# First layer's gated feed-forward: down products summed with tokens on partitions, and the embedding projection moved ahead of the gate

## The reference

```python
def gated_conv_ffn(u, w_up, conv_w, conv_b, w_down):
    up = u @ w_up
    a, g = up[..., :D_FF_2], up[..., D_FF_2:]
    a = causal_depthwise_conv(a, conv_w, conv_b)
    return (jax.nn.gelu(a, approximate=False) * g) @ w_down

    # one layer of the second block, D_FF_2 = 2816, PLE_DIM = 256
        u = rms_norm(h, attn_norm_w[i])
        proj = u @ w_in[i]
        ...
        h = h + mixed @ w_out[i]
        h = h + gated_conv_ffn(rms_norm(h, ffn_norm_w[i]), w_up[i], conv_w[i], conv_b[i], w_down[i])
        gate = jax.nn.sigmoid(rms_norm(h, ple_norm_w[i]) @ w_ple_gate[i])
        h = h + gate * (p[i] @ w_ple_proj[i])
```

## Time and profile before

| | value |
|---|---|
| median of 3 runs | 1278.66 us (1278.36 to 1279.01) |
| the profiled execution's own time | 1278.2 us |
| span from its first to its last instruction | 1276.5 us |
| granted TensorE clock, mean | 0.999 of 2.4 GHz |
| PE, DVE, ACT busy | 99%, 73%, 53% of the span |
| memory read | 228 MB, 180 GB/s over the span |

### The profile page before, as it was taken

The page is one execution under the profiler, slowest core; times in us unless marked ns, Lnnn a source line. Parts: engine busy times, 40 slices in busy tenths (PEclk is TensorE's granted clock), DMA queues, the critical chain, the costliest instruction groups (busy, mean ns, idle before and its releaser), DMA issues.

```text
span 1276.5 us, 20241 instructions
## 1 busy us (share of the span) xinstructions
PE 1267.4 (99%) x7932; PEld 1123.8 (88%) x7932; DVE 931.8 (73%) x1143; ACT 681.6 (53%) x808; POOL 32.6 (3%) x60
## 2 busy tenths in 40 slices
PE   9999999999999999999999999999999999999997
PEld 8988888888998888887889999999988898999996
DVE  5757765667667756658887888777877968877784
ACT  6646444446565444446655654444665556544455
POOL 0000000000132000000000000000000000000000
PEclk9999999999999999999999999999999999999999
DMA  9635655555433655554553455455455535554530
GB/s 377 243 129 220 232 184 189 197 197 196 139 128 133 242 191 184 182 190 169 203 165 133 165 183 200 179 196 186 177 173 192 172 132 182 198 192 175 194 133 33
DMA packets 34550, 232.44 MB, mean 182 GB/s; under 512 B 4016, under 2 KB 4272, under 8 KB 7344
## 3 DMA queue, kind: packets, MB, share of 16 engines
q1 hardware_dynamic: 30960, 218.90, 48.0%
q10 hardware_dynamic: 3520, 12.55, 3.0%
HBM read 228.29 MB, written 1.05 MB: 180 GB/s over the span
## 4 chain that ended last, share of the span: by engine, by line
PE 99%; DVE 0%; issue 0%; ACT 0%; DVEq 0%; ACTq 0%
PE ring L435 23%; PE ring L431 12%; PE ring L340 7%; PE ring L342 7%; PE ring L341 7%; PE acc L522 5%; PE acc L524 5%; PE acc L523 5%; PE acc L340 5%; PE acc L341 5%; PE acc L342 5%; PE acc L435 2%; PE ring L522 1%; PE ring L461 1%; PE ring L524 1%; PE ring L523 1%
## 5 line engine op out<-in xcount | busy, mean ns | idle before, releaser
L332 DVE TENSOR_TENSOR wlo<-raw,whi 128x2048 fp32r<-128x2048 f32 x203 | 463.8, 2290 | 86.1 <-ACT whi L324 85.4
L324 ACT CAST whi<-raw 128x2048 fp32r<-128x2048 f32 x200 | 381.6, 1909 | 79.8 <-PE acc L342 31.3
L435 PE MATMUL ring<-xs,whi 128*128 128x512 f32 x1280 | 320.5, 392 | 0.0
L435 PEld LDWEIGHTS ring<-xs,whi 128*128 128x128 f32 x1280 | 230.2, 189 | 41.2
L431 PEld LDWEIGHTS ring<-xs,wlo 128*128 128x128 f32 x1280 | 172.6, 190 | 12.5 <-issue 1.7
L431 PE MATMUL ring<-xs,wlo 128*128 128x256 f32 x1280 | 180.2, 284 | 0.0
L340 PE MATMUL ring<-xs,whi 128*128 128x256 f32 x512 | 148.0, 289 | 0.1
L341 PE MATMUL ring<-xs,whi 128*128 128x256 f32 x512 | 144.8, 283 | 0.0
L342 PE MATMUL ring<-xs,wlo 128*128 128x256 f32 x512 | 144.8, 283 | 0.0
L340 PE MATMUL acc<-hhi,whi 128*128 128x256 f32 x368 | 104.2, 283 | 0.0
L342 PE MATMUL acc<-hhi,wlo 128*128 128x256 f32 x368 | 104.1, 283 | 0.0
(11 more groups left out here) (370 smaller groups left out, 1825.0 us busy)
## 6 DMA issues: line engine op xcount, KB each, us to landing
raw<-wstream SPq DMA_DIRECT2D x206, 1024.0 KB, 4.9
sq<-lnp ACTq DMA_DIRECT2D x3, 1024.0 KB, 5.0
hT<-xT ACTq DMA_DIRECT2D x4, 256.0 KB, 5.7
raw<-wstream SPq DMA_DIRECT2D x4, 256.0 KB, 5.4
raw<-wstream SPq DMA_DIRECT2D x2, 512.0 KB, 8.6
hT<-xtok ACTq DMA_DIRECT2D x1, 1024.0 KB, 18.1
misc<-decay ACTq DMA_DIRECT2D x1, 1024.0 KB, 4.9
kT<-lnp ACTq DMA_DIRECT2D x1, 1024.0 KB, 4.9
```

What stands on the lines that cost most here:

```text
L324: act.copy(whi[:, c % SPLIT, :], raw[:, c % RAW, :]).then_inc(hi_made, 1)
L332: dve.tensor_tensor(wlo[:, c % SPLIT, :], raw[:, c % RAW, :], whi[:, c % SPLIT, :].bitcast(f32), ALU.subtract).then_inc(lo_made, 1)
L435: mm = pe.matmul(to(b + t), wh[:, w], xs[:, k, :, :].rearrange("p a s -> p (a s)"), start=False, stop=k == NT - 1, skip_group_check=True)
```

## The change

In layer 0 alone, the down products use `rows_half` into the four `acc` banks with tokens on partitions. The first product of each bank starts the bank itself, so ACT's clearing copy is left out. After the last down chunk ACT copies each of the four banks to `v`, and TensorE turns them by 16 transposes of 128x128 into ring banks 0 to 3, from which DVE adds to `hT`. The transposes are woven into the last chunk's products: three quarters of the product, eight transposes, the last quarter, eight transposes. The projection chunk comes ahead of the four gate chunks in the weight stream and on TensorE. TensorE's loop over the steps is cut at another place (1, then 2 to 5 and 6 to 9, then 10). Layer 1 keeps its form. The order of the operations on DVE and ACT between the layers stays the same but for the sources and semaphores.

```diff
@@ -32,8 +32,9 @@
 C_IN = [C_B2 + PER_B2 * n for n in range(DEPTH)]
 C_OUT = [c + 14 for c in C_IN]
 C_FFN = [c + 18 for c in C_IN]
-C_GATE = [c + 3 * N_FF for c in C_FFN]
-C_PROJ = [C_GATE[0] + 3, C_GATE[1] + 3]
+C_POST = [c + 3 * N_FF for c in C_FFN]
+C_GATE = [C_POST[0] + 1, C_POST[1]]
+C_PROJ = [C_POST[0], C_POST[1] + 3]
 C_END = [C_GATE[1] + j for j in (0, 1, 2, 4)]
 N_CHUNKS = C_B2 + PER_B2 * DEPTH
 
...
@@ -604,6 +604,37 @@
                         mm.then_inc(acc_done, 1)
                 mm.then_inc(chunk_used, 1)
 
+            def down_rows(c, s, mc, first):
+
+                pe.wait_ge(lo_made, mc + (c + 1))
+                for t in range(2):
+                    for half in range(2):
+                        mm = rows_half(1, c, t, half, hhi[:, s, :, :], hlo[:, s, :, :], first, False)
+                mm.then_inc(chunk_used, 1)
+
+            def last_down_rows(c, s):
+
+                def product(t, half):
+                    return rows_half(1, c, t, half, hhi[:, s, :, :], hlo[:, s, :, :], False, True)
+
+                def turned(t, half):
+                    pe.wait_ge(rows_kept, 2 * t + half + 1)
+                    for f in range(4):
+                        o = bank(2 * half + f // 2)[:, (f % 2) * 256 + t * 128:(f % 2) * 256 + t * 128 + 128]
+                        mm = pe.transpose(o, v[:, t, half * 512 + f * 128:half * 512 + f * 128 + 128], ident)
+                        if t and f % 2:
+                            mm.then_inc(rows_turned, 1)
+
+                pe.wait_ge(lo_made, c + 1)
+                product(0, 0).then_inc(ff_rows, 1)
+                product(0, 1).then_inc(ff_rows, 1)
+                product(1, 0).then_inc(ff_rows, 1)
+                for half in range(2):
+                    turned(0, half)
+                product(1, 1).then_inc(chunk_used, 1)
+                for half in range(2):
+                    turned(1, half)
+
             def squares_sum(n, o):
 
                 pe.wait_ge(sq_summed, n + 1)
@@ -626,8 +657,8 @@
 
                 pe.wait_ge(lo_made, c + 1)
                 pe.wait_ge(p_lo, L + 1)
+                pe.wait_ge(rows_kept, 4)
                 for j in range(4):
-                    pe.wait_ge(y_made, 4 * (2 + 3 * L) + j + 1)
                     for k in range(2):
                         for t in (2 * j, 2 * j + 1):
                             w = slice(k * D + t * 128, k * D + t * 128 + 128)
@@ -726,17 +757,23 @@
                     pe.wait_ge(g_sum, m * 4 + (b + i))
                     wide_gemm(ca + 1, 2, mc=m * 12)
                     pe.wait_ge(prod_lo, m * 4 + (b + i))
+                    if L == 0:
+                        down_rows(ca + 2, (i - 1) % 2, m * 12, i == 1)
+                        return
                     if i == 1:
-                        pe.wait_ge(acc_zero, ZERO[f"ffn{L}"] + 1)
+                        pe.wait_ge(acc_zero, 1)
                     down(ca + 2, (i - 1) % 2, mc=m * 12)
 
-                with pe.Fori(0, (N_FF - 1) // 4) as m:
-                    for i in range(1, 5):
+                step(1)
+                with pe.Fori(0, (N_FF - 3) // 4) as m:
+                    for i in range(2, 6):
                         step(i, m)
-                for i in range(N_FF - 2, N_FF):
-                    step(i)
+                step(N_FF - 1)
                 pe.wait_ge(prod_lo, b + N_FF)
-                down(c0 + 3 * N_FF - 1, (N_FF - 1) % 2, last=True)
+                if L == 0:
+                    last_down_rows(c0 + 3 * N_FF - 1, (N_FF - 1) % 2)
+                else:
+                    down(c0 + 3 * N_FF - 1, (N_FF - 1) % 2, last=True)
 
             def head(h):
                 return slice(64 * (h % 2), 64 * (h % 2) + 64)
@@ -1080,11 +1117,11 @@
                 ffn(L, X + 2)
                 if L + 1 == DEPTH:
                     break
+                ple_projection(C_PROJ[L], L)
                 for j in range(3):
                     gemm(C_GATE[L] + j, j, X + 3 if j == 0 else None,
                          between=(lambda: squares_sum(3 * L + 2, bank(3)[:, 0:S])) if j == 2 else None)
-                ple_projection(C_PROJ[L], L)
-                last_gate(C_GATE[L] + 4, L)
+                last_gate(C_GATE[L] + 3, L)
 
             def gate_rows(j, ts=(0, 1), between=None):
 
...
@@ -1374,8 +1411,9 @@
                 split_hi(act, c0 + 1 + AHEAD)
                 g_crossed(c0 + 1, 0)
                 split_hi(act, c0 + 2 + AHEAD)
-                act.copy(acc[:, :, :].rearrange("p t s -> p (t s)").rearrange("p (a b) -> p a b", b=128),
-                         wide(maskadd[:, 128:256], 16)).then_inc(acc_zero, 1)
+                if L:
+                    act.copy(acc[:, :, :].rearrange("p t s -> p (t s)").rearrange("p (a b) -> p a b", b=128),
+                             wide(maskadd[:, 128:256], 16)).then_inc(acc_zero, 1)
                 gelu(0)
                 high(0)
 
@@ -1394,6 +1432,10 @@
                         step(i, m)
                 for i in range(N_FF - 2, N_FF):
                     step(i)
+                if L == 0:
+                    for n, (t, half) in enumerate(((0, 0), (0, 1), (1, 0), (1, 1))):
+                        act.wait_ge(*((ff_rows, n + 1) if n < 3 else (chunk_used, c0 + 3 * N_FF)))
+                        act.copy(v_rows(t, half), acc_bank(2 * t + half)).then_inc(rows_kept, 1)
 
             def load_exp_ln():
 
...
@@ -1683,13 +1725,13 @@
                     act.activation(z, z, ACT.Sigmoid).then_inc(sig_made, 1)
 
                 def next_high(j):
-                    act.wait_ge(*((gate_passed, 3 * L + j + 1) if j < 3 else (chunk_used, C_GATE[L] + 5)))
+                    act.wait_ge(*((gate_passed, 3 * L + j + 1) if j < 3 else (chunk_used, C_GATE[L] + 4)))
                     weighted_high(3 * L + 3, "attn_w", 8 * L + 8, j)
 
                 for j in range(3):
                     gate_sigmoid(j)
                 for j in (3, 4):
-                    split_hi(act, C_GATE[L] + j + AHEAD)
+                    split_hi(act, C_POST[L] + j + AHEAD)
                 for j in range(3):
                     next_high(j)
                 gate_sigmoid(3)
...
@@ -1955,9 +1997,9 @@
                 else:
                     dve.wait_ge(chunk_used, c + 4)
 
-            def acc_ready(inst, c, j):
+            def acc_ready(c, j):
                 if j < 3:
-                    dve.wait_ge(acc_done, 3 * inst + j + 1)
+                    dve.wait_ge(acc_done, j + 1)
                 else:
                     dve.wait_ge(chunk_used, c + 1)
 
@@ -2365,19 +2407,22 @@
                 sum_squares(3 * L + 1)
                 ffn(L)
                 for j in range(4):
-                    acc_ready(ZERO[f"ffn{L}"], C_FFN[L] + 3 * N_FF - 1, j)
-                    add_to_h(j, pair(acc, j))
+                    if L:
+                        acc_ready(C_FFN[L] + 3 * N_FF - 1, j)
+                    else:
+                        dve.wait_ge(rows_turned, j + 1)
+                    add_to_h(j, pair(acc, j) if L else two(bank(j)))
                     if j:
                         weighted_low(X + 3, "ple_w", 8 * L, [j - 1])
                 weighted_low(X + 3, "ple_w", 8 * L, [3])
-                split_lo(dve, C_GATE[L] + AHEAD - 1)
-                split_lo(dve, C_GATE[L] + AHEAD)
+                split_lo(dve, C_POST[L] + AHEAD - 1)
+                split_lo(dve, C_POST[L] + AHEAD)
                 sum_squares(3 * L + 2)
                 if L + 1 == DEPTH:
                     break
 
                 def gate_scaled(j):
-                    dve.wait_ge(chunk_used, C_GATE[L] + (j + 1 if j < 3 else 5))
+                    dve.wait_ge(chunk_used, C_GATE[L] + j + 1)
                     if j == 0:
                         dve.wait_ge(rs_made, 3 * L + 3)
                     dve.tensor_tensor(pair(kT, j), two(bank(j)), wide(rs1, 2), ALU.mult).then_inc(z_scaled, 1)
...
@@ -2551,7 +2596,7 @@
         gate, proj = i["w_ple_gate_2"][n], _rows(i["w_ple_proj_2"][n])
         if n + 1 < DEPTH:
             gate = _cols(gate)
-            parts.extend([gate[0:3], proj, gate[3:4]])
+            parts.extend([proj, gate])
         else:
             gate = _wide_cols(gate)
             parts.extend([gate[0:3], proj, gate[3:4]])
```

More of the change, by code:

```diff
@@ L44 @@
 FREE = dict(gla_in=0, mlp0=12, sb_in=12 + N_UP, mlp1=24 + N_UP, in0=24 + 2 * N_UP, in1=38 + 2 * N_UP)
-ZERO = dict(ffn0=0, ffn1=1)
 H_OF = {1: 0, 7: 4, 11: 6}
@@ L173, in build_program @@
         xh_made, x_made, h_made = sem("xh_made"), sem("x_made"), sem("h_made")
-        y_made, mean_done, yc_made = sem("y_made"), sem("mean_done"), sem("yc_made")
+        y_made, mean_done, ff_rows = sem("y_made"), sem("mean_done"), sem("ff_rows")
         sq_made, var_done, rs_made = (sem(n) for n in ("sq_made", "var_done", "rs_made"))
@@ L188, in build_program @@
         xt_in, gb_in = sem("xt_in"), sem("gb_in")
-        h_turned, h_kept, end_half, end_pooled = (sem(n) for n in ("h_turned", "h_kept", "end_half", "end_pooled"))
```

(19 more changed lines are left out.)

## The result

The changed kernel takes 1283.51 us (median of 6 runs, 1282.74 to 1284.33), against 1278.45 us (6 runs) of the kernel before. The ratio is 1.004, with a 95% interval of 1.003 to 1.005: slower by 5 us. The profiled execution took 1282.74 us with a span of 1281.0 us, 4.5 us more than before, at a mean granted clock of 0.997 instead of 0.999. Three single executions among all runs of this text, far above the others of their kernels (1372.94, 2536.7 and 4231.98 us), are left out of every comparison.

What follows compares the result with a forecast made beforehand. TensorE's unbroken matmul stream was taken to bound the kernel. Terms of -3.1, +2.15 and +4.55 made +3.6 us on the profiled 1278.2, and with 0.46 added back about 1282.2 us; range 1279.5 to 1284.8.

Steps and rivals of the forecast that it cites:

- Down chunks by rows: Layer 0's down chunks 1 to 10: 24 matmuls of 512 columns save 0.31 us a chunk, -3.1 us in all.
- The last chunk: Last down chunk with its woven transposes: 7.9 us against 5.75 before, +2.15 us.
- the wait for ACT's last copy: Before the last four transposes: TensorE idles 0.6 to 0.7 us until ACT has copied the last quarter.
- Cover at the feed-forward's end: Before gate chunk 0: the moved projection's 5.75 us cover DVE's late adds and low parts, cost 0; without it near 2.5.
- The hole before layer 1: Behind the last gate chunk: TensorE waits for DVE's fixed queue to make the first low part, +4.55 us.
- The clock: Behind the idle time before layer 1: the point forecast took full clock as kept, chance 0.48.
- The rival with 1283.6 us: Before layer 1: TensorE's idle time also lets the clock fall, costing 1.4 us more; chance 0.22.
- the bound of 2.2 us: Matmuls at layer 1's start: most a fallen clock could lose, half rate for at most 4.4 us.
- The no-hole rival: Before layer 1: DVE is ready within the last gate chunk, -0.95 us, 1277.7 us; chance 0.20 with small holes or larger savings.

Runs made afterwards that it cites:

- the row form alone: The changed kernel with the projection put back between gate chunk 2 and the last gate chunk, down products by rows and transposes kept; 1279.06 us, ratio 1.0007.
- the old down form: The kernel before with only the projection moved ahead of the gate, down products still 48 matmuls with features on partitions; 1284.56 us, ratio 1.0049.
- the shorter hole: The changed kernel with DVE's second weight split before layer 1 moved behind the low parts of three pairs of layer 1's input; 1280.74 us, ratio 1.0013.
- the altered order: The changed kernel with one DVE weight split moved ahead of the gate's vector work, the next behind three low parts, ACT's casts likewise; 1277.23 us, ratio 0.9991.

## Why the prediction was right, point by point

The forecast was 1282.2 us, the measured time is 1283.5. The direction and the place of the loss were right, and the hole's length to 0.1 us. The one choice that was wrong is that the clock would hold. In the profiled execution the fall added 1.5 us, and 0.6 of them were hidden by three terms that came out better than forecast (the down chunks by 0.17, the last chunk by 0.30, the hole by 0.11 us). To that extent it is luck that the point forecast lies so near.

*Down chunks by rows.* Forecast -3.1, measured -3.27 up to the start of the last one: ten times 0.313, and the rest from a slightly shorter first chunk, the wide products between and a start that was 0.05 us earlier in that execution. By the Trainium skill ("TensorE: Matmul & The Clock Gate", "Back-to-back issue gap") the estimate for the ten chunks was a gain of 0.6 us. The measurement decides against it: the changed kernel has 0.227 us per matmul of 512 columns, like the MLP.

*The last chunk.* Forecast +2.15, measured +1.85. The mis-sized term is the wait for ACT's last copy. I put the hole at 0.65 us. The transposes stand 0.51 us apart at that place instead of 0.11, so it is 0.4. The other 0.1 lies in the transposes behind that wait, 0.41 us instead of 0.5. The way from ACT back to TensorE, which I had put at 0.2, was about 0.05 (ACT's copy runs from 897.70 for 0.59 us to 898.29, and the transposes begin at 898.34).

*Cover at the feed-forward's end.* Forecast 0, and gate chunk 0 followed the projection without idle. The price without that cover, which I put at near 2.5 us, is 1.6 us of idle time (1.9 by starts) in the kernel with the row form alone.

*The hole before layer 1.* Forecast 4.55, measured 4.44, and again 4.45 with the old down form. The steps held one by one: DVE's third scaling waits 0.55 us as before, the wait for the projection is gone, and ACT's cast comes early enough. The two splits stand in the queue at 2.28 us each.

*The clock.* I gave 0.48 to its holding and 0.22 to its falling. The rival with 1283.6 us was the case: +4.5 in the profiled execution and +5.1 between the medians. The step that failed is the weight between these two, not a mechanism. From the end of the kernel I read that the fall comes 4 to 4.5 us after the work stops, and took a hole of 4.5 us as one that only just reaches it. That row shows one case, not the shortest idle time that is enough. The runs have falls at 2.1 us of idle time (six of ten) and perhaps at 1.6 us (two of nine, by the mean clock and the time). In three of the four profiles with a fall it came only after work had begun again, by 0.2, 0.4 and 0.6 us. The price of 1.4 us was near the 1.5 and 1.7 in the two profiles, but the bound of 2.2 us does not hold: five of the eleven executions lost about 2.6. Its premise, that the low stretch lasts no longer than the clock took to fall, is false too: in the profile with the shorter hole the clock fell 2.7 us after the work had stopped and stayed at half rate for 3.4 us. The sentence of the Trainium skill ("TensorE: Matmul & The Clock Gate", "Why this matters for your kernels") on idle gaps spoke for this rival, and the trace after agrees with it, with a granted clock of 0.53 behind the hole. I should have given it more than half.

*The no-hole rival* was shown false for this change and true for the altered order, which makes its mechanism: 1277.2 us where it had said 1277.7.

## What to carry to other kernels

Work that needs nothing, like a projection of inputs, is cover, and it exists once. Before it is moved, count how long the queue of the next engine is at the place that it leaves, in its fixed order, and look in that engine's idle time for what could go ahead. Here the place of two weight splits of 2.3 us, of which one could run in 5 us of idle time, was the whole difference between 5 us lost and 1 us won. If a hole must remain, price the slower matmuls behind it too, even for a hole of 2 us. In this kernel, work that nobody needs, put into the hole, won back 1.8 of the 5 us.

## What was not expected of the hardware

By the mean clock, 2.1 us of idle time in TensorE's work cost the clock in six of ten executions of the same kernel, and a hole of 4.4 us in all fifteen that were made with it, over two kernels. With the hole filled by matmuls that nobody uses, and 0.6 us of it left, it fell in none of eight. The low stretch may begin before or after work starts again (the first distances behind the hole were 0.30 and 0.23 us in one kernel, 0.56 and 0.43 in another). The loss is 1.5 to 1.7 us in the profiles and about 1 us more in some executions. Why one execution keeps the clock and the next doesn't stays open.
